# A routed mixture-of-experts layer: gathered rows transposed in 32x32 blocks on VectorE, and the list work spread over more steps

## The reference

```
idx, w = route(h2, w_router, router_bias)          # top 8 of 64 experts per token
for each expert e:                                  # rows of the tokens that chose e
    y = (silu(h2[tok] @ w_gate[e]) * (h2[tok] @ w_up[e])) @ w_down[e]
    acc[tok] += y * w
x = x + acc + swiglu(h2, w_sh_gate, w_sh_up, w_sh_down)
x = x + sigmoid(rmsnorm(x) @ w_ple_gate) * rmsnorm(p @ w_ple_proj)
```

## Time and profile before

| | |
|---|---|
| median of three runs | 989.62 us (988.42 to 990.00) |
| span of the profiled execution, first to last instruction | 986.4 us |
| busy of that span | PE 932.8 us (95%), DVE 360.1 us (37%), POOL 226.8 us (23%), ACT 162.6 us (16%) |
| DMA | 301.04 MB, mean 305 GB/s |
| share of the span on the chain that ended last | PE 74%, DMA 20%, DVE 2%, SP queue 2% |

### The profile page before, as it was taken

How to read it: one execution, slowest core, us unless ns; L and a number is a source line. 1 busy time by engine, 2 the same in 40 slices (tenths; PEclk the granted TensorE clock), 3 DMA queues, 4 the chain that set the end, 5 groups by cost and what they waited for, 6 DMA issues and landing times.

```text
span 986.4 us, 15652 instructions
## 1 busy us (share of the span) xinstructions
PE 932.8 (95%) x6359; PEld 483.9 (49%) x6359; DVE 360.1 (37%) x773; ACT 162.6 (16%) x304; POOL 226.8 (23%) x344
## 2 busy tenths in 40 slices
PE   6999999999999999999999999989979889897798
PEld 4678788888655533333333333344323333332344
DVE  5565673336436733333332110111101111111687
ACT  2001324210011211111111111111101102121021
POOL 4115923162100112222222222212121211201110
PEclk9999999999999999999999999999989999999899
DMA  9940005421482699999999999999999999999972
GB/s 331 331 129 1 1 1 184 158 86 63 143 317 107 223 385 386 407 418 395 411 420 407 398 422 410 408 422 415 397 422 421 421 421 419 419 401 373 380 270 85
DMA packets 83912, 301.04 MB, mean 305 GB/s; under 512 B 9299, under 2 KB 35959, under 8 KB 59648
## 3 DMA queue, kind: packets, MB, share of 16 engines
q1 hardware_dynamic: 70144, 263.19, 67.8%
q0 software_dynamic: 11920, 33.63, 8.8%
q10 hardware_dynamic: 1776, 3.21, 0.9%
HBM read 279.26 MB, written 29.36 MB: 313 GB/s over the span
## 4 chain that ended last, share of the span: by engine, by line
PE 74%; DMA 20%; SPq 2%; DVE 2%; issue 1%; ACT 1%; POOL 0%; ACTq 0%; POOLq 0%
PE ps L2223 22%; DMA ring<-in_w_exp_up 18%; PE ps L1826 12%; PE ps L2252 8%; PE ps L1976 6%; PE ps L1955 5%; PE ps L2367 4%; PE ps L1782 3%; PE ps L1759 2%; PE ps L2047 1%; PE ps L1788 1%; DMA ring<-accumulator 1%; PE ps L2232 1%; DMA accumulator<-actT,stage 1%; SPq L525 1%; PE ps L1875 1%
## 5 line engine op out<-in xcount | busy, mean ns | idle before, releaser
L2223 PE MATMUL ps<-ring,gates 128*32 128x512 f32 x2560 | 289.3, 604 | 26.1 <-DMA ring<-in_w_exp_up 25.3
L2223 PEld LDWEIGHTS ps<-ring,gates 128*32 128x32 f32 x2560 | 88.8, 111 | 218.6 <-issue 217.7
L2252 PE MATMUL ps<-ring,poolbuf 128*32 128x512 f32 x1280 | 145.6, 595 | 3.1 <-DMA ring<-in_w_exp_down 3.1
L1573 DVE COPY poolbuf<-ps 128x256 f32<-128x256 f32 x40 | 17.0, 424 | 355.4 <-PE ps L2232 355.4
L791 POOL TENSOR_TENSOR tickets<-cst 128x1 f32<-128x1 f32 x77 | 14.5, 188 | 397.1 <-ACT actT L991 391.7
L2252 PEld LDWEIGHTS ps<-ring,poolbuf 128*32 128x32 f32 x1280 | 37.9, 109 | 83.5 <-issue 81.9
L991 ACT ACTIVATE actT<-ps,qT 128x1024 f32<-128x1024 f32 x40 | 44.5, 1113 | 142.3 <-PE ps L2252 142.3
L983 ACT ACTIVATE poolbuf<-ps 128x256 f32<-128x256 f32 x40 | 15.4, 384 | 280.0 <-PE ps L2223 280.0
L1826 PE MATMUL ps<-xrow,ring 128*128 128x256 f32 x256 | 57.9, 381 | 0.1
L1976 PE MATMUL ps<-ring,gates 128*128 128x512 f32 x128 | 56.4, 594 | 0.0
L1759 PE MATMUL ps<-cst,rows 128*128 128x128 f32 x352 | 47.6, 281 | 8.3 <-DVE rows L1087 8.3
(11 more groups left out here) (294 smaller groups left out, 1062.3 us busy)
## 6 DMA issues: line engine op xcount, KB each, us to landing
ring<-in_w_exp_down SPq DMA_DIRECT2D x64, 1024.0 KB, 17.6
ring<-in_w_exp_gate SPq DMA_DIRECT2D x62, 1024.0 KB
ring<-in_w_exp_up SPq DMA_DIRECT2D x62, 1024.0 KB
ring<-accumulator SPq DMA_DIRECT2D x12, 1024.0 KB, 13.1
ring<-in_w_gate SPq DMA_DIRECT2D x8, 1024.0 KB, 13.2
ring<-in_w_in SPq DMA_DIRECT2D x5, 1024.0 KB, 12.9
xrow<-in_x SPq DMA_DIRECT2D x8, 512.0 KB, 5.1
accumulator<-ring SPq DMA_DIRECT2D x1, 4096.0 KB, 19.9
```

The source lines that it names most:

```text
L2223: last = mm(bank(2 + k)[part, :], hgT[k][:, q, part], pair_view(EXPERT_SLOT[js[c]])[:, q], start=(q == 0), stop=(q == KD - 1))
L2252: last = mm(bank(6 + half)[part, :], eactT[r % 2][:, q, part], w[:, q, half * 512:(half + 1) * 512], start=(q == 0), stop=(q == 1))
```

## The change

The eight PE transposes of the gathered rows, and the two copies out of PSUM, are kept only for step 0. For steps 1 to 39, `block_T(r)` on DVE transposes the gathered rows straight from `hg` to `hgT` in 32x32 blocks: 16 `nc.vector.transpose` operations (each of four quadrants of columns for each of four strips of rows), each of 32 partitions by 256 elements. `block_T(r + 1)` stands first in DVE's step r, ahead of `act_T(r - 1)` and `act_rows(r)`; it waits for the gather of step r + 1 and for `up(r - 1)`. `up(r)` on PE and the next gather on POOL wait for `blocks_ready` in place of the semaphores of the old transposes. The list work of groups 1 to 15 moves from steps 1 to 15 to steps 1, 2, 4, 5, 7, 8, 10, 12, 13, 15, 16, 18, 19, 21 and 23 (`LIST_STEP`).

```diff
--- before.py
+++ after.py
@@ -56,6 +56,7 @@
 LCOL = TCOL + 2 * WCOL
 LATE = (2, 3)
 SMALL_AT = GROUP * CAP * BIG_GROUPS // P
+LIST_STEP = [0] + [1 + 22 * (g - 1) // 14 for g in range(1, NGROUP)]
 JOB_STEP = [SMALL_AT + n // 2 for n in range(8)] + [SMALL_AT + 6 + n // 2 for n in range(4 * NT)]
 
 
@@ -338,7 +339,7 @@
         ticket_done = [sem(f"ticket_done{n}") for n in range(2)]
         gathered = [sem(f"gathered{j}") for j in range(BUF)]
         scattered = [sem(f"scattered{j}") for j in range(BUF)]
-        hgT_ps, hgT_lo_ready, hgT_hi_ready = sem("hgT_ps"), sem("hgT_lo_ready"), sem("hgT_hi_ready")
+        hgT_ps, first_T_ready, blocks_ready = sem("hgT_ps"), sem("first_T_ready"), sem("blocks_ready")
         gu_ps, silu_ready, eact_ready = sem("gu_ps"), sem("silu_ready"), sem("eact_ready")
         eactT_ps, eactT_ready = sem("eactT_ps"), sem("eactT_ready")
         y_ps, y_ready = sem("y_ps"), sem("y_ready")
@@ -813,7 +814,10 @@
 
 
                 if not last:
-                    pool.wait_ge(hgT_ps, 2 * r + 2)
+                    if r:
+                        pool.wait_ge(blocks_ready, r)
+                    else:
+                        pool.wait_ge(hgT_ps, 2)
                     stage_from(r + BUF, j)
                     if not first:
                         pool.wait_ge(ticket_done[0], r)
@@ -972,12 +976,6 @@
                                      scale=st[:, 1, i:i + 1]).then_inc(shared_silu, 1)
 
 
-            def rows_hi(r, k):
-
-                act.wait_ge(hgT_ps, 2 * r + 2)
-                nc.scalar.activation(hgT[k][:, 4:8, :], bank(1).rearrange("p (k n) -> p k n", k=4),
-                                     ACT.Copy).then_inc(hgT_hi_ready, 1)
-
             def silu(r, k):
                 act.wait_ge(gu_ps, STRIPS * (r + 1))
                 nc.scalar.activation(esilu[k], bank(2 + k)[:, 0:FE], ACT.Silu).then_inc(silu_ready, 1)
@@ -1007,15 +1005,15 @@
             shared_silu_of(0)
             act.wait_ge(hgT_ps, 1)
             nc.scalar.activation(hgT[0][:, 0:4, :], bank(0).rearrange("p (k n) -> p k n", k=4),
-                                 ACT.Copy).then_inc(hgT_lo_ready, 1)
-            rows_hi(0, 0)
+                                 ACT.Copy).then_inc(first_T_ready, 1)
+            act.wait_ge(hgT_ps, 2)
+            nc.scalar.activation(hgT[0][:, 4:8, :], bank(1).rearrange("p (k n) -> p k n", k=4),
+                                 ACT.Copy).then_inc(first_T_ready, 1)
             shared_silu_of(1)
             for r in range(STEPS):
                 if r == STEPS - 3:
                     longest = longest_list(act)
                 silu(r, r % 2)
-                if r + 1 < STEPS:
-                    rows_hi(r + 1, (r + 1) % 2)
                 for n in jobs_of(r, 0):
                     job(n)
                 if r == STEPS - 1:
@@ -1558,10 +1556,20 @@
                 at = (g % 2) * 64
                 return bank(5)[:, at:at + LCOL * steps_of(g)].rearrange("p (s c) -> p s c", c=LCOL)
 
-            def rows_T(r, k):
-                dve.wait_ge(hgT_ps, 2 * r + 1)
-                nc.vector.tensor_copy(hgT[k][:, 0:4, :], bank(0).rearrange("p (k n) -> p k n", k=4)
-                                      ).then_inc(hgT_lo_ready, 1)
+            def block_T(r):
+
+
+                j, k = r % BUF, r % 2
+                dve.wait_ge(gathered[j], 16 * (r // BUF + 1))
+                if r >= 2:
+                    dve.wait_ge(gu_ps, STRIPS * (r - 1))
+                for q in range(STRIPS):
+                    for c in range(STRIPS):
+                        rows_c = hg[j][c * STRIP:(c + 1) * STRIP, q * 256:(q + 1) * 256]
+                        last = nc.vector.transpose(
+                            hgT[k][q * STRIP:(q + 1) * STRIP, :, c * STRIP:(c + 1) * STRIP],
+                            rows_c.rearrange("p (d k) -> p k d", k=KD))
+                last.then_inc(blocks_ready, 1)
 
             def act_rows(r, k):
                 dve.wait_ge(silu_ready, r + 1)
@@ -1601,19 +1609,20 @@
             for r in range(STEPS):
                 if r == STEPS - 3:
                     longest = longest_list(dve)
+                if r + 1 < STEPS:
+                    block_T(r + 1)
                 if r:
                     act_T(r - 1, (r - 1) % 2)
                 act_rows(r, r % 2)
-                if r + 1 < STEPS:
-                    rows_T(r + 1, (r + 1) % 2)
-                if 1 <= r < NGROUP:
-                    dve.wait_ge(list_ps, r + 1)
-                    rows_of(r, found_of(r))
-                    if r == 1:
+                if r in LIST_STEP[1:]:
+                    g = LIST_STEP.index(r)
+                    dve.wait_ge(list_ps, g + 1)
+                    rows_of(g, found_of(g))
+                    if g == 1:
                         weights_of(0, found_of(0))
-                    weights_of(r, found_of(r))
-                    if r + 1 < NGROUP:
-                        places(r + 1, rank3[:, :, (r + 1) * GROUP:(r + 2) * GROUP])
+                    weights_of(g, found_of(g))
+                    if g + 1 < NGROUP:
+                        places(g + 1, rank3[:, :, (g + 1) * GROUP:(g + 2) * GROUP])
                 for n in jobs_of(r, 0) + jobs_of(r, 1):
                     if n < 6 and n % 3 < 2:
                         late_T(n // 3, n % 3)
@@ -2185,23 +2194,18 @@
                 last.then_inc(ple_ps, 1)
 
 
-            def rows_T(r):
-
-
-                j = r % BUF
-                pe.wait_ge(gathered[j], 16 * (r // BUF + 1))
-                if r:
-                    pe.wait_ge(hgT_lo_ready, r)
-                    pe.wait_ge(hgT_hi_ready, r)
-                else:
-                    pe.wait_ge(ssq2_done, NT)
-                strided_T(hg[j], None, 0, P, hgT_ps)
+            def first_rows_T():
+                pe.wait_ge(gathered[0], 16)
+                pe.wait_ge(ssq2_done, NT)
+                strided_T(hg[0], None, 0, P, hgT_ps)
 
             def up(r):
                 g, s = STEP_OF[r]
                 k = r % 2
-                pe.wait_ge(hgT_lo_ready, r + 1)
-                pe.wait_ge(hgT_hi_ready, r + 1)
+                if r:
+                    pe.wait_ge(blocks_ready, r)
+                else:
+                    pe.wait_ge(first_T_ready, 2)
                 if r == 1:
                     pe.wait_ge(shared_act, 2)
                 js = [strip_expert(g, s, c) for c in range(STRIPS)]
@@ -2266,7 +2270,7 @@
                 else:
                     ple_proj(n - 8 - 2 * NT)
 
-            rows_T(0)
+            first_rows_T()
             shared_up(1, 4, 8)
             for r in range(STEPS):
                 if r == STEPS - 3:
@@ -2274,10 +2278,8 @@
                 up(r)
                 if r:
                     acts_T(r - 1)
-                if r + 1 < STEPS:
-                    rows_T(r + 1)
-                if 1 <= r < NGROUP:
-                    lists(r)
+                if r in LIST_STEP[1:]:
+                    lists(LIST_STEP.index(r))
                 for n in jobs_of(r, 0):
                     job(n)
                 if r:
```

## The result

The changed kernel takes 1067.77 us (median of 4 runs, 1066.01 to 1070.85), the kernel before 989.81 us beside it: a ratio of 1.079 (95% interval 1.077 to 1.081), 78 us. The forecast was 990.5 us with a range of 986 to 996; the result lies far above it, on the side of the slower rivals and beyond all of them.

The account below looks back on a forecast made before the run. The prediction took the DMA engines to bound the steps: span 986.4 us + 1.2 (start) - 0.35 (tail) + 0 (steps) = 987.3, with the runs' median 3.2 above the span giving 990.5 us, range 986.0 to 996.0.

Parts of the forecast that it names:

- the slower rivals: Whole run: slow strided block transposes, 998 us, chance 0.13; full start loss plus longer step 2 stall, 991.3 to 993.3, 0.15.
- What bounds the kernel: Steps: DMA needs 12.75 us each in the first eight groups, PE 12.34, so relieving PE of 34 us gains 0.
- The price of a block transpose: On DVE: 0.35 us per operation, taken from copies; bounds 0.30 (1.18 ns an element) and 0.60 us.
- T: Time of one block_T, a step's 16 block transposes on DVE: 5.6 us forecast, bounds 4.8 and 9.7.
- The loop of two steps: Gather, landing, block_T, then down until up(r + 3): 23.8 us per two steps, 11.9 a step, faster than DMA's 12.75.
- L: Time from a gather's issue to its landing: 6.0 to 9.9 us in the forecast, 9.9 in its loop sum.
- Rival 3: Strided block transposes take 0.6 us, T = 9.7; start loses 5 us, loop 3.3: 998 us, chance 0.13.
- The threshold L + T = 17.2: In the loop of two steps: from this sum in us on, the loop decides instead of DMA's 12.75 a step.
- The start: First block_T makes up(1) 2.0 us late, on a nearly dry DMA queue; 1.2 us of it counted as lost.
- The further stall at up(3): Step 2: block_T(3) waits for gather 3, act_T(1) comes 2 to 6 us late; free, the queue holding 10 us.
- Lists: DVE's list work spread over steps 1 to 23: costs nothing, group 15 listed in step 23 for step 38.
- Late steps: Last eight groups: DMA needs 17.6 us a step against PE's 11.8, so DMA bounds without doubt.

Follow-up runs that it names:

- one block: The changed kernel with one of the 16 block transposes of a step, the other 15 left out: 987.0 us, ratio 0.998 to the kernel before.
- contiguous reads: The changed kernel with each block transpose reading 256 contiguous floats of a row instead of every eighth one: 1020.5 us, ratio 1.032 to the kernel before.
- early gather: The changed kernel with POOL issuing the gather of step r + 3 ahead of the scatter of step r - 1: 1041.4 us, ratio 1.053.
- after: The changed kernel itself, against the kernel before: 1067.77 us, ratio 1.079; its profiled execution took 1070.85 us.
- eight blocks: The changed kernel with 8 of the 16 block transposes of a step: 993.6 us, ratio 1.0041 to the kernel before.
- packed rows and early gather: The changed kernel with h2 rows stored plane by plane, read in runs of 32 floats, and the gather ahead of the scatter: 996.4 us, ratio 1.0073.

## Why the prediction was wrong, point by point

**What bounds the kernel.** Right. With one block PE is relieved of all its transposes and the time moves by 1.6 us; the forecast's 0.35 us for the tail and nothing for the steps was close enough.

**The price of a block transpose.** The first step that failed. I took 0.35 us, with an upper bound of 0.60, and it is 0.65: T is 10.3 us and not 5.6, above my bound of 9.7. With it DVE's own sum, 10.5 us in a step with a list by the forecast, is about 15, above DMA's 12.75. Two errors add up. I took the spacing of copies, which overlap by 0.08 us, for an operation that doesn't overlap with its like; and I held PE's indifference to the stride, and the length of the copies, for evidence about DVE. The first is 0.1 us of the error (contiguous reads are 0.45 apart), the second 0.2. The operations behind the 1.18 ns of my lower bound read float32 but write bfloat16, though the text ahead calls all numbers float32; the bound came out near the 1.1 ns. The Trainium skill, "SBUF — State Buffer", section "Specifications (TRN2)", with its two hits per 16-byte line, agrees with what DVE shows (1.9 against 1.1 ns an element), though PE shows nothing of it. I gave that rival 0.13.

**The loop of two steps.** The loop was right, and I argued its price away. "Two steps are 8.3 + L + T" holds where DVE stands waiting for the gather: with T = 10.3 and L = 10.8 us it gives 29.4 us, and in the chain above down(5) to down(7) take 475.90 - 446.21 = 29.7 us. PE's timeline:

```profile
446.21 3.64 PE L2256 MATMUL ps<-ring,poolbuf 128*32 128x512 f32 x32 [1.97 <-DVE poolbuf L1581]
...
475.90 5.37 PE L2256 MATMUL ps<-ring,poolbuf 128*32 128x512 f32 x32 [5.98 <-DVE poolbuf L1581]
...
490.65 3.64 PE L2256 MATMUL ps<-ring,poolbuf 128*32 128x512 f32 x32 [2.08 <-DVE poolbuf L1581]
```

But the pattern has three steps, not two. The third one, the 14.75 us to down(8), is no gather's: DVE does act_T, act_rows, the list and the next 16 blocks without waiting from 475.22 to 489.94. From up(8) to up(11) (469.0 and 512.9 us) a step takes 14.6 us. That this is also half of the loop's 29.4 is chance.

Rival 3 had the same loop at 14.0 a step and 1.25 us above DMA's need, and then shortened L to 6.0 us "as soon as DMA has less to do" and counted a third of a microsecond for ten steps. L does fall: of the 21 gathers for steps 3 to 23, 13 land within 8.4 us and 8 take 10.2 to 11.4 (mean 7.6). The shortest of all 40 is below that of rows 9, while the median and the longest are nearly the same:

```profile
DMA to landing us min/median/max: 4.2/10.0/11.4
```

With the mean of 7.6 the loop would take 13.1 us a step, and measured are 14.5 from up(3) to up(24), so the loop alone is not the price. What rival 3 left out is that an early landing is of no use while DVE, which works in order, is still at the step before: gather 10 lands at 472.3 and its blocks begin at 479.35. Where DVE does wait, the loop holds again. A stall comes in about every third step; here is one from down(13) to down(15), 30.3 us for two steps (chain):

```profile
559.82 3.74 PE ps L2256 x32
...
567.67 11.41 DMA rows<-h_rows,stage
...
590.10 6.29 PE ps L2256 x32
```

The loss is 2.3 us in each of 21 steps and not a third of a microsecond in ten. The threshold L + T = 17.2 was in the text: with T = 5.6, L = 9.9 it is missed by 1.7 us only, and contiguous reads (T = 7.2, L to 11) are over it. The early gather takes L out of the loop and gives back 26 us (T = 10.3) and 27 us (T = 7.2). Of the 48 us that after loses in steps 4 to 24, 25 go with it; 23 stay, and most of them are DVE's own sum (a few slow `down`s are left too). So T and L are both causes: with T at 7.2 us DVE has time enough in each step, and the kernel still loses 34 us while act_T stands behind a gather. The other way out, act_T ahead of block_T on DVE, was not run, so what that order would give is open.

**A term that was missing: slower matmuls after a wait.** `down` of 3.74 us becomes 6.29 us right after a wait of 6.95 us for act_T. Its line in PE's timeline, and the two windows of after that cover it, with the columns of rows 2:

```profile
590.10 6.29 PE L2256 MATMUL ps<-ring,poolbuf 128*32 128x512 f32 x32 [6.95 <-DVE poolbuf L1581]
...
590.00:593.00 3.00, 2.90 (x16) 0.92 (x20) 2.76 (x14) 0.00 (x0) 0.00 (x0) 0.50 0.79 330
593.00:597.00 4.00, 4.00 (x28) 1.10 (x24) 3.92 (x8) 0.47 (x1) 0.00 (x0) 0.69 0.11 41
```

The granted clock is 0.50, the level of 1.2 GHz, in the first 3 us and 0.69, a mix of 1.2 and 2.4 GHz, in the rest, where the DMA share falls to 0.11: PE slow, the transfer queue dry. Not every wait does this, and the length of the wait alone does not tell: after 2.08 us `down` takes its usual 3.64, after 5.98 us 5.37 (rows above), and with early gather 6.55 after only 3.01:

```profile
468.89 6.55 PE L2261 MATMUL ps<-ring,poolbuf 128*32 128x512 f32 x32 [3.01 <-DVE poolbuf L1586]
```

Over the run PE is busy 180.3 us with `down` in place of 145.6, 35 us more, and `down` is a part of the loop. The forecast knew the 8.76 us of a late `up`, and it foresaw a wait of PE at the start, but put no slower matmuls into any sum. What share of the 78 us this is can't be read off but for the start, since no run took the clock apart from the waits.

**The start.** The wait was right, its size was not, and what follows a wait was missing. up(1) was to be 2.0 us late and 1.2 of it to stay. By the same sum with T = 10.3 it starts at 347.8 + 10.3 = 358.1 us, and it does start at 358.04, 6.6 us late. The rest is the missing term: it takes 9.70 us in place of 7.07, with a granted clock of 0.50 in its first 4 us, and ends 9.2 us late. (up(1) in PE's timeline, and three windows with the columns of rows 2.)

```profile
358.04 9.70 PE L2227 MATMUL ps<-ring,gates 128*32 128x512 f32 x64 [8.36 <-DVE gates L1569]
...
358.00:360.00 2.00, 1.96 (x12) 0.59 (x16) 1.96 (x4) 0.00 (x0) 0.00 (x0) 0.50 0.83 338
360.00:362.00 2.00, 2.00 (x12) 0.38 (x8) 1.96 (x4) 0.00 (x0) 0.00 (x0) 0.50 0.18 74
...
364.00:368.00 4.00, 4.00 (x38) 1.17 (x31) 3.92 (x7) 0.11 (x1) 0.00 (x0) 1.00 0.00 0
```

With eight blocks up(1) starts 1.5 us late and takes 8.77, with packed rows and early gather it starts 3.9 us late and takes 9.92. The other runs show that nearly all of the delay stays: 3.2 us at up(1) and 4.1 at the end for eight blocks, 6.7 and 6.9 for packed rows with early gather, and 0.2 us and -1.1 with PE's transposes kept in steps 1 to 3. The queue in front of up(1)'s release had next to nothing in reserve: in after nothing at all is moved from 364 to 368 us. The steps that failed are the guess of 1.2 between 0 and 2.0, and the slower matmuls that were put at nothing. The further stall at up(3), "visible on PE and free for the end", is 16.1 us in after; in packed rows with early gather it is 10.4 us, of which 3.5 are won back later, so that it is nearly free holds there, and not for T = 10.3.

**Lists.** Right as far as it was tried: with the block transposes of after the time is the same, spread or not.

**Late steps.** Counted at nothing, since DMA needs 17.6 us there against PE's 11.8; DVE's T, act_T and act_rows are 11 us even with T = 10.3. With T = 7.2 us that holds (36.2 us of loss at step 39 against 40.3 at step 24); with T = 10.3 another 20 us are lost, 12 with early gather. The cause of these is open. The jobs of those steps go back and forth between PE and DVE behind block_T, which may be it, but no run took the jobs away.

## What to carry to other kernels

Moving work off an engine that looks full is worth what the next bound leaves, here 1.6 us of 34; a run that drops nearly all of the moved work tells that first. An operation put at the head of an in-order engine brings its own wait with it: follow that wait (gather, landing, transpose, the copy behind it, the scatter that precedes the next gather) as a closed loop, and divide by the steps that it spans. Then add up that engine's own work in a step as well, with the same price, and believe both quotients unless a row shows that they are wrong. Where a price comes from a neighbour's row, ask whether the neighbour overlaps with itself and reads with the same stride.

## What the runs showed of the hardware

- An operation that transposes float32 in 32x32 blocks on VectorE, 32 partitions by 256 elements, takes 0.436 us with contiguous reads, and the same with runs of 32 floats, and 0.637 us when it reads every eighth float. Consecutive ones don't overlap: they start 0.45 and 0.65 us apart. An estimate from three spacings is 0.17 us fixed and 1.1 or 1.9 ns an element.
- An indirect gather of 128 rows of 4 KB lands 10 to 11 us after its issue where the DMA engines are full (11.4 us from 567.7 us on, share 1.02). The shortest, 4.2 us from 485.5 us on, ran beside a share of 0.72.
- After a wait of 7 us PE ran 32 matmuls in 6.29 us that take 3.64 us otherwise, at a granted clock of 0.50 and then 0.69. The same 32 took 5.37 us after 5.98, 6.55 after 3.01, and 3.64 after 2.08.
